# W2's sums on a schedule of their own with two buffer sets, and activation variants stored in two parts, in layer one of a fused decoder step

## What is computed

```python
def post_block(x, mix, ln1_g, ln1_b, w1, w2, ln2_g, ln2_b):
    x = layer_norm(ALPHA * x + mix, ln1_g, ln1_b)
    h = jnp.square(jax.nn.relu(x @ w1)) @ w2
    return layer_norm(ALPHA * x + h, ln2_g, ln2_b)
```

## Time and profile before

| | us |
|---|---|
| three executions | 1337.77, 1340.78, 1342.85 (median 1340.78) |
| the profiled execution | 1341.03 |
| its span | 1339.0 |
| TensorE matmul busy | 1254.1 (94% of the span) |
| VectorE busy | 835.0 (62%) |
| ScalarE busy | 561.7 (42%) |
| mean granted TensorE clock | 0.973 of full speed |
| DMA, bytes moved | 226.89 MB, mean 169 GB/s |

### The profile page before, as it was taken

How to read it: one execution, slowest core, us unless ns; L and a number is a source line. 1 busy time by engine, 2 the same in 40 slices (tenths; PEclk the granted TensorE clock), 3 DMA queues, 4 the chain that set the end, 5 groups by cost and what they waited for, 6 DMA issues and landing times.

```text
span 1339.0 us, 24463 instructions
## 1 busy us (share of the span) xinstructions
PE 1254.1 (94%) x9650; PEld 1184.9 (88%) x9650; DVE 835.0 (62%) x1324; ACT 561.7 (42%) x925; POOL 174.1 (13%) x217
## 2 busy tenths in 40 slices
PE   7999999999789997999997999999999999999896
PEld 7987777899667776999987999999998999999896
DVE  4122212345797776566887777777758666668878
ACT  3212223234744445554753444444463333333325
POOL 3524333110000000023000000000000000000653
PEclk9999999999898999999998999999999999999898
DMA  8749888433320011431345775676697555554003
GB/s 291 231 130 297 280 280 282 120 111 95 120 49 11 10 64 47 129 99 59 103 154 201 260 281 219 240 270 239 247 324 277 180 189 190 190 190 164 27 12 116
DMA packets 110710, 226.89 MB, mean 169 GB/s; under 512 B 12755, under 2 KB 60133, under 8 KB 106502
## 3 DMA queue, kind: packets, MB, share of 16 engines
q1 hardware_dynamic: 104454, 208.56, 45.5%
q0 software_dynamic: 6144, 16.79, 4.0%
HBM read 165.54 MB, written 58.73 MB: 167 GB/s over the span
## 4 chain that ended last, share of the span: by engine, by line
PE 64%; DVE 14%; DMA 6%; SPq 5%; ACT 5%; issue 4%; POOLq 1%; POOL 0%; ACTq 0%; DVEq 0%
PE psum L2736 18%; PE psum L2387 17%; PE psum L355 9%; PE psum L1910 5%; PE psum L1341 3%; SPq L267 2%; PE psum L2938 2%; SPq L270 2%; PE psum L1672 2%; DMA hid_rows<-hid_variants 1%; DMA step_hid_first<-hid_rows 1%; DVE softmax_stats L1747 1%; PE psum L1688 1%; DVE y_sums L2762 1%; DMA x_mean<-scratch 1%
## 5 line engine op out<-in xcount | busy, mean ns | idle before, releaser
L2736 PE MATMUL psum<-step_hid_hi,step_w_hi 128*128 128x258 f32 x784 | 160.3, 286 | 7.7 <-DVE y_sums L2787 3.6
L2736 PE MATMUL psum<-step_hid_hi,step_w_lo 128*128 128x258 f32 x784 | 159.2, 285 | 0.0
L2736 PE MATMUL psum<-step_hid_lo,step_w_hi 128*128 128x258 f32 x784 | 158.8, 284 | 0.0
L355 PE MATMUL psum<-xTh,win_hi 128*128 128x344 f32 (+1 forms) x432 | 147.7, 342 | 9.7 <-DVE xTl L408 9.7
L355 PE MATMUL psum<-xTl,win_hi 128*128 128x344 f32 (+1 forms) x432 | 139.3, 323 | 0.0
L355 PE MATMUL psum<-xTh,win_lo 128*128 128x344 f32 (+1 forms) x432 | 139.2, 322 | 0.0
L2736 PEld LDWEIGHTS psum<-step_hid_hi,step_w_hi 128*128 128x128 f32 x784 | 123.9, 193 | 8.2 <-issue 3.8
L2736 PEld LDWEIGHTS psum<-step_hid_hi,step_w_lo 128*128 128x128 f32 x784 | 122.8, 192 | 0.0
L2736 PEld LDWEIGHTS psum<-step_hid_lo,step_w_hi 128*128 128x128 f32 x784 | 122.7, 192 | 0.0
L2387 PE MATMUL psum<-x_t_hi,w_variant_hi 128*128 128x258 f32 x512 | 105.2, 287 | 12.5 <-DVE product_sums L2481 11.6
L2387 PE MATMUL psum<-x_t_lo,w_variant_hi 128*128 128x258 f32 x512 | 105.1, 287 | 0.0
(11 more groups left out here) (405 smaller groups left out, 3006.0 us busy)
## 6 DMA issues: line engine op xcount, KB each, us to landing
hid_rows<-hid_variants SPq DMA_DIRECT2D x14, 1806.0 KB, 6.9
step_hid_raw<-hid_rows SPq DMA_DIRECT2D x21, 1032.0 KB, 7.5
k_pages<-in_pages SPq DMA_DIRECT2D x128, 160.0 KB, 3.0
v_pages<-in_pages POOLq DMA_DIRECT2D x128, 128.0 KB, 4.4
w_raw<-in_w SPq DMA_DIRECT2D x16, 1024.0 KB, 5.1
step_w_raw<-w_sums SPq DMA_DIRECT2D x12, 1024.0 KB, 5.2
step_w_raw<-in_w SPq DMA_DIRECT2D x9, 1024.0 KB, 5.2
win_raw<-in_w_in SPq DMA_DIRECT2D x17, 512.0 KB, 6.8
```

The source lines that it names most:

```text
L355: mm = pe.matmul(psum[0:M, 3 * (m % 2) + b, 0:BLK], w[:, m % 2, k, 0:M], x[:, k, b * BLK:(b + 1) * BLK], start=(k == 0 and i == 0), stop=( ...
L2736: mm = pe.matmul(slot(d)[:, s, :], wt[r][:, w], ht[r][:, TH * f + s * BW:TH * f + (s + 1) * BW], start=(f == 0 and i == 0), stop=(f == G - ...
```

## The change

Four edits, all in layer one.

1. W2's sums no longer hang on the turns. `W2_SUM_AT` places one block every 5.5 products, beginning at the P6 of turn 4. In that slot come the first two of its four sums, in the next slot the other two. Odd blocks have buffers of their own (`w2three`, `w2fourth`, in space that the early products no longer use), with semaphores of their own; a block is stored two slots after its first sums, and its buffers loaded again three slots after that.
2. The seven variants are stored in two parts: five (B11, B12, B22, T2, T3) after T2, in two DMAs, and two (B21, T4) after T4, in one. `hv_free` now waits for the first part, and only the write of B21 waits for the second.
3. In turns 1 to 3, T3 and T1 move from the slot of P6 to that of P5, T2 from P7 to P4, T4 from P4 to P3.
4. In turns 1 to 3, ScalarE's `square11` moves from behind the turn's first product to behind P5.

```diff
--- before.py
+++ after.py
@@ -1827,7 +1827,10 @@
         aff_done, xv_hi, xv_lo, xt_done = (sem(n) for n in ("x1_affine", "x_variant_hi", "x_variant_lo", "x_variant_summed"))
         zs_stored, zb_loaded, w1early_loaded, ONE_IN = x_loaded[3], x_loaded[4], x_loaded[5], 16
         st_loaded, PAGES_IN = kp_loaded, 16 * PG * NU // 2
-        hv_stored, w2_loaded, w2s_stored, GLA_ROWS_IN = gv_loaded, gqk_loaded[0], gqk_loaded[1], 16 * 4
+        hvb_stored, HVB_IN, hva_done, HVA_IN = (duv_loaded, gst_loaded), (16 * 1, 16 * 4), gr_ones, 1
+        hv_stored, GLA_ROWS_IN = gv_loaded, 16 * 4
+        w2_loaded, W2L_IN = (gqk_loaded[0], xm_stored), (16 * 4, 16)
+        w2s_stored, W2S_IN = (gqk_loaded[1], pt_loaded), (16 * 4, 16)
         VAR_BANK = psum[:, 7, 0:BW]
 
 
@@ -2231,6 +2234,8 @@
         hv = sb(PERSIST, "hid_variants", [P, 14, TH])
         w2low = sb(PERSIST + 7224, "w2_left_half", [P, 2, 512])
         w2up = sb(AREA + 25272, "w2_right_half", [P, 2, 512])
+        w2three = sb(AREA + 26304, "w2_odd_three", [P, 3, 512])
+        w2fourth = sb(AREA + 28368, "w2_odd_fourth", [P, 512])
         assert 7224 + 1024 <= KD * T
 
         mwa_hi, mwa_lo, ws_done, pa_mm = (sem(n) for n in ("variant_hi", "variant_lo", "w1_variant_summed", "product_done"))
@@ -2404,7 +2409,7 @@
         def hv_free(eng, n):
 
             if n >= 2:
-                eng.wait_ge(hv_stored[n % 2], GLA_ROWS_IN + 16 * (n // 2))
+                eng.wait_ge(hv_stored[n % 2], GLA_ROWS_IN + 32 * (n // 2))
             else:
                 eng.wait_ge(xv_lo, len(XV_LO))
                 eng.wait_ge(zs_stored, ONE_IN + 96)
@@ -2440,8 +2445,8 @@
             if p == turn_order(n)[0]:
                 if n:
                     square(act, n - 1, HV_B12)
-                if n < NE:
-                    square11(act, n)
+            if p == "P5" and n < NE:
+                square11(act, n)
             if p == "P2":
                 hidden11(act, n)
                 square11(act, n)
@@ -2499,6 +2504,8 @@
             if p in ("P4", "P3"):
                 dve.wait_ge(pa_mm, c + 1)
                 h = h_view(n, HV_B21 if p == "P4" else HV_B12)
+                if p == "P4" and n >= 2:
+                    dve.wait_ge(hvb_stored[n % 2], HVB_IN[n % 2] + 16 * (n // 2))
                 dve.tensor_tensor(two(h), slot(slot_of(n, p)), two(u23[:, 0, :]), ALU.add).then_inc(u_c_done, 1)
 
         def hid_t3_t1(dve, n):
@@ -2511,11 +2518,12 @@
         def hid_t2(dve, n):
 
             t1, b22, t2 = (h_view(n, v) for v in (HV_B12, HV_B22, HV_T2))
-            dlink(dve, dve.tensor_tensor(t2, b22, t1, ALU.subtract))
+            dve.tensor_tensor(t2, b22, t1, ALU.subtract).then_inc(hva_done, 1)
 
         def hid_t4(dve, n):
 
             b21, t2, t4 = (h_view(n, v) for v in (HV_B21, HV_T2, HV_T4))
+            dve.wait_ge(hva_done, HVA_IN + n + 1)
             dve.tensor_tensor(t4, b21, t2, ALU.subtract).then_inc(hv_done, 1)
 
         def dve_hidden(dve):
@@ -2543,35 +2551,54 @@
                 if c + 4 < NPROD:
                     w1_lo(dve, c + 4)
                 dve_w1_sums(dve, c + 5)
-                if 0 < n <= NW and p == "P6":
+                if 0 < n <= NW and p == ("P5" if n < NE else "P6"):
                     hid_t3_t1(dve, n - 1)
-                if 0 < n <= NW and p == "P7":
+                if 0 < n <= NW and p == ("P4" if n < NE else "P7"):
                     hid_t2(dve, n - 1)
-                if 0 < n <= NW and p == "P4":
+                if 0 < n <= NW and p == ("P3" if n < NE else "P4"):
                     hid_t4(dve, n - 1)
-                if n >= 2 and p in turn_order(n)[:3]:
-                    w2_sums(dve, n - 2, turn_order(n).index(p))
+                w2_sums(dve, c)
                 dve_prep_at(dve, c)
             dve_after(dve, NPROD - 1)
 
+        W2_SUM_AT = {AT[NE, "P5"] + 1 + 11 * q // 2: q for q in range(NW)}
+
+        def w2_quarters(q):
+            if q % 2:
+                return [w2three[:, 0, :], w2three[:, 1, :], w2three[:, 2, :], w2fourth[:]]
+            return [w2low[:, 0, :], w2low[:, 1, :], w2up[:, 0, :], w2up[:, 1, :]]
+
+        def w2_parts(q):
+            return ((slice(0, 3), w2three[:]), (slice(3, 4), w2fourth[:].unsqueeze(1))) if q % 2 else ((slice(0, 2), w2low[:]), (slice(2, 4), w2up[:]))
+
         def load_w2(sp, q):
-
-            if q:
-                sp.wait_ge(w2s_stored, GLA_ROWS_IN + 32 * q)
-            else:
+            if q == 0:
                 sp.wait_ge(sq_done, 1)
                 sp.wait_ge(u_c_done, u2_at(1))
-            for half, t in ((0, w2low), (1, w2up)):
-                sp.dma_start(t[:], a["w2"][q, :, 2 * half:2 * half + 2, :]).then_inc(w2_loaded, 16)
+            elif q == 1:
+                sp.wait_ge(sq_done, 4 * NE)
+                sp.wait_ge(u_c_done, u2_at(2))
+            else:
+                sp.wait_ge(w2s_stored[q % 2], W2S_IN[q % 2] + 32 * (q // 2))
+            for v, t in w2_parts(q):
+                sp.dma_start(t, a["w2"][q, :, v, :]).then_inc(w2_loaded[q % 2], 16)
 
         def store_w2(sp, q):
             sp.wait_ge(ws2_done, q + 1)
-            for half, t in ((0, w2low), (1, w2up)):
-                sp.dma_start(w2s[q, :, 2 * half:2 * half + 2, :], t[:]).then_inc(w2s_stored, 16)
-
-        def store_hid(sp, n):
+            for v, t in w2_parts(q):
+                sp.dma_start(w2s[q, :, v, :], t).then_inc(w2s_stored[q % 2], 16)
+
+        def store_hid_early(sp, n):
+            rows = hvs[n].rearrange("p (v c) -> p v c", v=7)
+            sp.wait_ge(hva_done, HVA_IN + n + 1)
+            for v in (slice(HV_B11, HV_B21), slice(HV_B22, HV_T4)):
+                sp.dma_start(rows[:, v], hv[:, 7 * (n % 2) + v.start:7 * (n % 2) + v.stop, :]).then_inc(hv_stored[n % 2], 16)
+
+        def store_hid_late(sp, n):
+            rows = hvs[n].rearrange("p (v c) -> p v c", v=7)
             sp.wait_ge(hv_done, n + 1)
-            sp.dma_start(hvs[n].rearrange("p (v c) -> p v c", v=7), hv[:, 7 * (n % 2):7 * (n % 2) + 7, :]).then_inc(hv_stored[n % 2], 16)
+            sp.dma_start(rows[:, HV_B21:HV_T4 + 1:HV_T4 - HV_B21], hv[:, 7 * (n % 2) + HV_B21:7 * (n % 2) + HV_T4 + 1:HV_T4 - HV_B21, :]
+                         ).then_inc(hvb_stored[n % 2], 16)
 
         def load_z(sp, i, p, ks, c):
             if i:
@@ -2579,34 +2606,45 @@
             sp.dma_start(acc_of(p), zs[:, ks, c]).then_inc(zb_loaded, 16)
 
         def sp_hidden(sp):
-            for n in range(NP - 1):
-                if n + 2 < NP:
-                    sp.wait_ge(mwa_lo, AT[n, "P3"] + 1)
-                    load_w1(sp, n + 2)
-                if n >= 2:
-                    store_w2(sp, n - 2)
-                if n:
-                    load_w2(sp, n - 1)
-                    store_hid(sp, n - 1)
-            sp_step_load(sp, 1)
-            sp_step_load(sp, 0)
-            store_w2(sp, NW - 1)
+            for n in range(NP):
+                for p in turn_order(n):
+                    c = AT[n, p]
+                    if p == "P6" and n + 2 < NP:
+                        sp.wait_ge(mwa_lo, AT[n, "P3"] + 1)
+                        load_w1(sp, n + 2)
+                    if 0 < n <= NW and p == ("P4" if n < NE else "P7"):
+                        store_hid_early(sp, n - 1)
+                    if 0 < n <= NW and p == ("P3" if n < NE else "P4"):
+                        store_hid_late(sp, n - 1)
+                    if (n, p) == (NE - 1, "P3"):
+                        load_w2(sp, 0)
+                    if (n, p) == (NE, "P7"):
+                        load_w2(sp, 1)
+                    if c - 2 in W2_SUM_AT:
+                        store_w2(sp, W2_SUM_AT[c - 2])
+                    if c - 5 in W2_SUM_AT and W2_SUM_AT[c - 5] + 2 < NW:
+                        load_w2(sp, W2_SUM_AT[c - 5] + 2)
+                    if (n, p) == (NP - 1, "P1"):
+                        sp_step_load(sp, 1)
+                        sp_step_load(sp, 0)
             sp_step_load(sp, 2)
             sp.wait_ge(u_c_done, u2_at(NP - 1))
+            sp.wait_ge(w2s_stored[0], W2S_IN[0] + 32 * (NW // 2))
+            sp.wait_ge(w2s_stored[1], W2S_IN[1] + 32 * (NW // 2))
             load_z(sp, 0, "P5", XHALF[1], slice(TH, T))
-            sp.wait_ge(w2s_stored, GLA_ROWS_IN + 32 * NW)
             load_z(sp, 1, "P3", XHALF[0], slice(TH, T))
 
-        def w2_sums(dve, q, part):
-
-            a11, a12, a21, a22 = w2low[:, 0, :], w2low[:, 1, :], w2up[:, 0, :], w2up[:, 1, :]
-            if part == 0:
-                dve.wait_ge(w2_loaded, GLA_ROWS_IN + 32 * (q + 1))
+        def w2_sums(dve, c):
+
+            if c in W2_SUM_AT:
+                q = W2_SUM_AT[c]
+                a11, a12, a21, a22 = w2_quarters(q)
+                dve.wait_ge(w2_loaded[q % 2], W2L_IN[q % 2] + 32 * (q // 2 + 1))
                 dlink(dve, dve.tensor_tensor(a22, a21, a22, ALU.add))
                 dlink(dve, dve.tensor_tensor(a21, a11, a21, ALU.subtract))
-            elif part == 1:
+            if c - 1 in W2_SUM_AT:
```

(5 more changed lines are left out.)

## The result

| | before | with the change |
|---|---|---|
| median of the runs, us | 1340.61 (4 runs, 1337.77 to 1342.85) | 1332.29 (4 runs, 1331.48 to 1333.49) |
| ratio, 95% interval | | 0.9936, 0.9916 to 0.9957 |
| the profiled execution, us | 1341.03 | 1331.96 |
| its span, us | 1339.0 | 1328.6 |
| mean granted TensorE clock | 0.973 | 0.979 |

The change is faster by 0.6%, 8.3 us. The forecast was 14.8 us, and 1332.29 lies 0.8 us above the range of 1321.0 to 1331.5: the direction was right, the size was not.

What follows compares the result with a forecast made beforehand. TensorE, 94% busy, was taken to lose time waiting, mainly for u3 in turns 1 to 3, and to clock drops. -14.7 + 0.8 - 0.9 = -14.8 us gave 1326.2 by the profile, 1326.0 us median; range 1321.0 to 1331.5.

Steps and rivals of the forecast that it cites:

- Turns 1 to 3: Layer one, first matmul of turn 1 to first of turn 4: 46.15 us instead of 60.82, -14.7 us.
- W2's sums in the seven-product turns: Layer one from turn 4: sums ahead of u3 delay P4 in two turns by about 0.4 us each, +0.8 us.
- The turn 4 pause: Layer one, P4 of turn 4: u3, eleven places behind the low split, makes a new pause of about 0.4 us.
- The start of layer two: Layer two's first steps: loads come about 2 us earlier and the 0.9 us wait goes, -0.9 us.
- Short pauses cost clock: Pauses at P4 of turns 1, 4 and 11 each cost 1.74 us of clock: 1331.2 us; chance 10%.
- The stores are still late: Turns 2 or 3: a store landing of 11.33 us stalls ScalarE again, 1327 to 1330 us; chance 7%.
- Layer two gains more: Layer two: the 3.2 us wait of step 6 and a 1.74 us clock loss go: 1321.1 us; chance 13%.
- step 6's wait: Layer two: TensorE's 3.2 us wait hangs on step 7's load, which the change does not touch; left as is.
- Slower: Seven-product turns: late u3 costs 3.0 us in each of 12 turns, 36 us, 1362 us; chance 3%.
- The change doesn't do what it says: Turns 1 to 3: low splits, not u3, held TensorE; little but the store's chain (9.9) moves: 1330.9 us; chance 5%.

Runs made afterwards that it cites:

- the five blocks of an experiment: The changed kernel with W2's blocks at other offsets, five of them in the slots of P4 and P3 ahead of c12; one run, 1330.40 us.

## Why the prediction came out as it did

**Turns 1 to 3: right.** 45.96 us against 46.15. u2 and u3 of turn 1 come where the count of places put them (u3 at 689.33, forecast 689.95, with turn 1 starting 0.34 earlier):

```profile
687.28 0.69 DVE L2480 TENSOR_TENSOR product_sums<-psum,first_products 128x516 f32<-128x516 f32 x1
...
689.33 0.69 DVE L2486 TENSOR_TENSOR product_sums<-psum,product_sums 128x516 f32<-128x516 f32 x1
```

The pause is 1.10 us, forecast 1.3, with the clock at 1.00. The waits at the P4 of turns 2 and 3 are gone, as is `square11`'s. The experiments divide the stage: 11.55 us for the W2 work taken out, 3.6 for T3, T1, T2 and T4 (the pause and its clock); the two overlap a little, and `square11`'s place and the store in two parts add nothing that these turns show.

**W2's sums in the seven-product turns: wrong, the step that failed.** The text put +0.8 us, two pauses of 0.4 at the P4 of turns 4 and 11, with bounds 0 and 1.6. It measured +4.77, which is 3.97 of the 5.76 us by which the profiled execution missed its forecast of 1326.2. The sentence that fails is "In the other positions at most two of the four sums lie there, which is today's case, without a pause." It looks at u3 alone, and two sums were today's case in turn 4 only: a full turn had one behind the split. c12 is the same kind of consumer, at the other end of the turn: P5 waits for it, it too stands behind a low split that waits for ScalarE, and the earlier trace rows had a wait of 0.9 us for it already. Two blocks fall ahead of it and cost 1.18 and 1.17 us plus their restarts, the five blocks of an experiment 1.26 each. That is 2.35 of the 3.97. For turn 11 the mechanism was right and the size off: 1.12 instead of 0.4, because I took the start of the low split from turn 4, +3.85, where it is +4.61 in a full turn. The trace of the kernel before had it at +4.73 in its turn 8 (827.21, P5 at 822.48). Turn 4 had the early split since its P5 had just waited: in turn 10, whose P5 waits as well, it is at +3.83. And the two blocks in the slots of P5 and P6 put two sums ahead of the split and two behind it, where before the change it was one and one: 0.26 and 0.27. The turn 4 pause, 0.28, was nearly as worked out.

**The start of layer two: no gain shown.** The forecast was -0.9. The first trace has -0.48, but the same kernel's second trace takes 39.15 us, as long as the kernel before (39.16), so the -0.48 is within what executions differ by. "W2's last store comes in turn 14" was true of its sums, but the queue held it until 0.4 us behind the activation store. Step 0's load therefore lands 7.5 us before the first matmul of layer two, and 8.4 in the second trace, against 7.6 before the change (974.07 and 981.66); with the last block three slots earlier it is 10.9. Step 2's wait, 0.9 us before, is 0.59 and 0.83. Across ten traces the stretch takes 37.72 to 37.98 us where the last W2 store is early (four of them) and 38.68 to 39.56 where it is late (six); the two kernels with one activation store, 40.55 and 40.87, are left out. The forecast's 0.9 was thus there to be had (the early ones are 1.2 to 1.4 us below the kernel before), but not with this order of the queue.

**The rivals.** *Short pauses cost clock*: it did not come true. Its time of 1331.2 is near the measured one, and for the wrong reason. The granted clock was 1.00 behind every pause of 0.88 to 1.35 us in layer one, also five times in a row, one every 41.8 us. The Trainium skill ("TensorE: Matmul & The Clock Gate", section "A second HAM failure mode: psum-queue depth-cycling") has frequent short idle spells make the clock swing; these rows do not show it. *The stores are still late*: no, ScalarE waits for none. *Layer two gains more*: no, step 6's wait is 3.01 us in the change and 2.88 to 3.57 in the experiments, whatever lies ahead of it. It hangs on step 7's load, as the prediction says: the load takes 8.5 to 8.9 us, ScalarE's and VectorE's splits for step 7 wait for it and stand ahead of the sums (`y_sums`) that TensorE waits for, and TensorE goes on 15.8 to 16.1 us after the load's issue in all 13 traces. *Slower*: its mechanism, u3 late, appeared in four turns instead of twelve, with 0.26 to 1.12 us each instead of 3.0. *The change doesn't do what it says*: no.

What stays open: how much of the 3 us wait of step 6 an earlier load of step 7 would take away, which no run tried, and what is left of the 5.76 us: 0.42 in layer two's start, 0.51 in the rest of the span and 1.33 outside it, with 0.5 the other way ahead of turn 4. No run addressed these, and they are no more than executions differ by.

## To carry to other kernels

Where filler work (sums that nobody is waiting for) is put into an in-order engine's list, list every result of that engine that another one waits for and count the places between each and the last thing that holds it back, for every phase in which the filler can fall. A period that does not divide the turn (5.5 against 7 products) visits all of them, the worst ones too. The same count holds for a DMA queue: what a transfer is worth early depends on the wait in front of it, and a small transfer ahead of a critical load is better than a large one.

## What the runs showed of the hardware

- **Short pauses were free of clock, longer ones mostly not.** Behind pauses of TensorE of 0.88 to 1.35 us in layer one the granted clock was 1.00 (2.4 GHz) in every trace. Behind pauses of 2.57, 2.93, 3.10 and 3.23 us there it was 0.53, 0.64, 0.52 and 0.56 over some 3.4 us, thus mostly the 1.2 GHz level. No pause in layer one lies between 1.35 and 2.57 us, so where it turns is open. The length of the pause alone does not decide it: behind step 6's wait of layer two, 2.88 to 3.57 us, the clock fell in 11 of 13 traces and stayed at 1.00 in two, behind 3.13 and 3.38 us.
- **A 512 KB load behind a store of 1806 KB** on the same queue landed in 8.4 and 9.2 us (two loads, issued within 0.9 us of the store), behind one of 516 KB in 5.0 and 5.6 us.
- **Whole-program times scatter more than stages.** Turn 1 starts between 677.34 and 683.23 us in the traces of kernels with the same code up to there, while turns 4 to 15 without pauses take 240.30 or 240.31 us in every one. The length of a stage in one trace decided what the medians of repeated runs could not.
